# The up product of a two-layer feed-forward by Strassen's scheme: seven half-size products per strip in place of eight

## The reference, cut to what matters

```
h   = modulate(rms_norm(x), shift, scale)          # tokens x 1024
u   = h @ w_up                                      # 1024 x 5632: 2816 values, 2816 gates
u   = conv3(u)                                      # 3 taps along the tokens, per channel, zero at the ends
hid = value * silu(gate)                            # tokens x 2816
x   = x + gate_mod * (hid @ w_down)                 # 2816 x 1024
```

## Time and profile before

| | |
|---|---|
| median of 3 runs | 2685.11 us (2683.37 to 2685.4) |
| profiled execution | 2683.82 us, its span 2682.0 us |
| mean granted TensorE clock | 0.993 of full |
| TensorE busy | 2615.8 us, 98% |
| VectorE, ScalarE, GpSimd busy | 904.6, 613.0, 53.0 us |
| share of the chain that ended last | PE 95%, of the up loop (L1235) 15% |

### The profile page before, as it was taken

How to read it: one execution, slowest core, us unless ns; L and a number is a source line. 1 busy time by engine, 2 the same in 40 slices (tenths; PEclk the granted TensorE clock), 3 DMA queues, 4 the chain that set the end, 5 groups by cost and what they waited for, 6 DMA issues and landing times.

```text
span 2682.0 us, 29803 instructions
## 1 busy us (share of the span) xinstructions
PE 2615.8 (98%) x11774; PEld 1764.1 (66%) x11774; DVE 904.6 (34%) x1530; ACT 613.0 (23%) x1103; POOL 53.0 (2%) x42
## 2 busy tenths in 40 slices
PE   7999999999999899899999999999999999999999
PEld 3556656656656587666886444864444587889888
DVE  2236365365365512354125111232222014113321
ACT  3122212222121112243214000122221013113321
POOL 0000000000000100000000000000000000000000
PEclk9999999999999999999999999999999999999999
DMA  8443343333333223112520223222225232353572
GB/s 312 161 166 126 110 156 121 129 141 109 126 125 79 76 73 111 54 30 73 141 63 1 63 63 94 63 63 78 76 70 133 65 79 64 94 180 87 154 201 68
DMA packets 319714, 280.26 MB, mean 104 GB/s; under 512 B 27617, under 2 KB 298601, under 8 KB 319513
## 3 DMA queue, kind: packets, MB, share of 16 engines
q1 hardware_dynamic: 317882, 274.89, 33.4%
q0 software_dynamic: 1280, 4.20, 0.4%
q10 hardware_dynamic: 479, 0.13, 0.0%
HBM read 278.15 MB, written 1.05 MB: 104 GB/s over the span
## 4 chain that ended last, share of the span: by engine, by line
PE 95%; DVE 2%; DMA 1%; ACT 1%; SPq 0%; issue 0%; ACTq 0%; DVEq 0%
PE ps L660 17%; PE ps L1235 15%; PE ps L1158 9%; PE ps L1261 4%; PE ps L1251 4%; PE ps L669 4%; PE ps L707 4%; PE ps L1194 3%; PE ps L1170 3%; PE ps L427 2%; PE ps L853 2%; PE ps L807 2%; PE ps L789 2%; PE ps L374 2%; PE ps L1008 2%; PE ps L1221 1%
## 5 line engine op out<-in xcount | busy, mean ns | idle before, releaser
L660 PE MATMUL ps<-hT,ring_mem 128*128 128x512 f32 x1024 | 455.1, 598 | 1.7 <-ACT hT L440 1.7
L1235 PE MATMUL ps<-hT,ring_mem 128*128 128x512 f32 (+1 forms) x1280 | 413.2, 486 | 2.5 <-DMA ring_mem<-in_w_up_dram 2.5
L1235 PEld LDWEIGHTS ps<-hT,ring_mem 128*128 128x128 f32 x1280 | 243.1, 190 | 171.8 <-issue 155.3
L660 PEld LDWEIGHTS ps<-hT,ring_mem 128*128 128x128 f32 x1024 | 190.9, 191 | 234.8 <-issue 232.5
L1158 PE MATMUL ps<-hT,ring_mem 128*128 128x512 f32 (+1 forms) x768 | 250.3, 486 | 0.0
L1158 PEld LDWEIGHTS ps<-hT,ring_mem 128*128 128x128 f32 x768 | 145.9, 190 | 101.3 <-issue 91.4
L1986 DVE SCALAR_TENSOR_TENSOR arena<-ps,vecs,arena 128x510 f32<-128x510 f32 (+1 forms) x176 | 100.2, 611 | 304.6 <-ACT arena L1602 298.2
L707 PEld LDWEIGHTS ps<-arena,K_c 128*128 128x128 f32 x896 | 116.2, 194 | 34.3 <-issue 20.1
L707 PE MATMUL ps<-arena,K_c 128*128 128x128 f32 x896 | 120.1, 289 | 9.1 <-ACT K_c L1405 9.0
L1949 DVE TENSOR_TENSOR arena<-ps,arena 128x512 f32<-128x512 f32 (+1 forms) x48 | 26.8, 558 | 291.2 <-PE ps L1170 291.2
L1261 PE MATMUL ps<-arena,ring_mem 128*128 128x256 f32 (+1 forms) x704 | 116.1, 327 | 0.0
(11 more groups left out here) (246 smaller groups left out, 3090.5 us busy)
## 6 DMA issues: line engine op xcount, KB each, us to landing
ring_mem<-in_w_mod_dram SPq DMA_DIRECT2D x24, 2048.0 KB, 7.7
ring_mem<-in_w_up_dram SPq DMA_DIRECT2D x88, 512.0 KB, 4.9
ring_mem<-in_hg_w_in_dram SPq DMA_DIRECT2D x40, 1024.0 KB, 5.0
ring_mem<-in_w_in_dram SPq DMA_DIRECT2D x30, 1024.0 KB, 5.4
ring_mem<-in_w_down_dram SPq DMA_DIRECT2D x16, 1408.0 KB, 7.4
ring_mem<-in_ada_w_dram SPq DMA_DIRECT2D x8, 2048.0 KB, 7.8
ring_mem<-in_mla_w_in_dram SPq DMA_DIRECT2D x9, 1024.0 KB, 5.4
ring_mem<-in_hg_w_out_dram SPq DMA_DIRECT2D x8, 1024.0 KB, 12.0
```

Source lines behind the costliest of these rows:

```text
L660: mm = PE.matmul(bank, wj[:, k, m * 128:m * 128 + 128], hT[:, k, :], start=k == 0, stop=k == 7)
L1235: mm = PE.matmul(ps[:, 2 * j + m, 0:n], wj[:, k, m * 128:m * 128 + 128], hT[:, k, c0:T], start=k == 0, stop=k == 7)
```

## The change

For each strip the 1024 x 256 weights are cut into four blocks: a11 (input tiles k 0 to 3, values), a12 (k 4 to 7, values), a21 (k 0 to 3, gates), a22 (k 4 to 7, gates). The activations are cut in the same way: channels k 0 to 3 or 4 to 7, token half a or b. Seven products of half the depth and half the columns (P1 to P7, 4 matmuls each) replace the 16 matmuls over all tokens. Four of them take sums of weight blocks (S_up, two buffers), three differences of activations (T_up); hT's own tiles 0 to 3 of half b are overwritten by a difference.

- Activations: VectorE makes the four differences once per layer, when half b is ready (up_turned_vector).
- Weights: the sums 0 and 2 of strip f come from VectorE (first_sums, 4 x 128 columns each), for strips 0 and 1 from GpSimd; sums 1 and 3 always from GpSimd.
- Results: ScalarE copies P1 out of PSUM (into root), VectorE gathers the seven into the strip's values and gates, C_up (in SBUF, two buffers) by six additions. The middle and the outer taps then read C_up.
- Order: TensorE does P1 and P2 of strip f (plain), P4, P7, P5, P6, P3 (summed), and may be two strips ahead of the gathering (c_ready). VectorE's turn f is: first sums of f+2, gathering of f, taps of f-1, hidden of f-2. ScalarE's: copy P1 of f, taps of f, sigmoid of f-1; its taps of f wait for hidden f-2.
- Loops of up are written out for all engines. up has 4 slots at words 4096 to 12287 (loads on semaphores 2 to 5) in place of 2, so its slots 0 and 1 lie where out's slots 2 and 3 do.
- The banks of down's first pass are 0 to 3 (before 4 to 7), those of the halves are swapped, and the norms' sums of half b move to bank 7, so their squares wait for all of out's additions. The next layer's first keys wait for an addition of down more.

```
+        if s["total"] < s["slots"] * s["turns"]:
+            for n in range(s["total"]):
+                t, j = divmod(n, s["slots"])
+                if t or s["need"][j]:
+                    sp.wait_ge(self.used, s["first"] + n - s["slots"] + 1 if t else s["need"][j])
+                for dst, src in copies(j, t):
+                    sp.dma_start(dst, src).then_inc(self.loaded[s["first_slot"] + j], 16)
+            return
...
+        S_up = at(2 * 4 * 512).rearrange("p (b s k n) -> p b s k n", b=2, s=4, k=4)
+        T_up = at(3 * 4 * 256).rearrange("p (s k t) -> p s k t", s=3, k=4)
+        U_up = at(3 * 256).rearrange("p (s t) -> p s t", s=3)
+        P1_up = root
...
-            ring.stage(f"up{l}", 2, 2048, FT // 2, [2] * 2, first_slot=4, at=8192)
+            ring.stage(f"up{l}", 4, 2048, 6, [2] * 4, first_slot=2, at=4096, total=FT)
...
-            pe.wait_ge(x_added, x_part(l, "out", part, 1))
+            pe.wait_ge(x_added, x_part(l, "out", part, 1 if part == "_a" else 7))
...
+        def up_region(f, name, hw):
+            bank, part = {"P1": (0, 0), "P6": (0, 1), "P2": (1, 0), "P7": (1, 1), "P4": (2, 0), "P5": (2, 1), "P3": (3, 0)}[name]
+            return ps[:, f % 2 * 4 + bank, part * hw:part * hw + hw]
...
+            a, b, hw = up_halves(l)
+            def product(f, which, left, right, ready=None):
+                for k in range(4):
+                    if ready:
+                        ready(k)
+                    mm = PE.matmul(up_region(f, which, hw), left[:, k, :], right[:, k, 0:hw], start=k == 0, stop=k == 3)
+                return mm
+            def plain(f):
+                t, j = divmod(f, 4)
+                ring.wait_loaded(pe, name, j, t)
+                if f >= 2:
+                    pe.wait_ge(c_ready, FT * l + f - 1)
+                wj = strip(name, j, 8)
+                product(f, "P1", wj[:, 0:4, 0:128], hT[:, 0:4, a], (lambda k: wait_h(pe, f"ffn{l}_a", k)) if f == 0 else None)
+                product(f, "P2", wj[:, 4:8, 0:128], hT[:, 4:8, a], (lambda k: wait_h(pe, f"ffn{l}_a", 4 + k)) if f == 0 else None)
+            def summed(f):
+                wj = strip(name, f % 4, 8)
+                sums = S_up[:, f % 2]
+                p4 = lambda: product(f, "P4", wj[:, 4:8, 128:256], T_up[:, 2])
+                if f >= 1:
+                    p4()
+                if f >= 2:
+                    pe.wait_ge(first_sums_ready, (FT - 2) * l + f - 1)
+                else:
+                    pe.wait_ge(sums_ready, FT * l + f + 1)
+                if f == 0:
+                    pe.wait_ge(turned_ready, 4 * l + 1)
+                product(f, "P7", sums[:, 2], T_up[:, 0])
+                if f == 0:
+                    pe.wait_ge(turned_ready, 4 * l + 2)
+                product(f, "P5", sums[:, 0], hT[:, 0:4, b])
+                pe.wait_ge(sums_ready, FT * l + f + 1)
+                if f == 0:
+                    pe.wait_ge(turned_ready, 4 * l + 3)
+                product(f, "P6", sums[:, 1], T_up[:, 1])
+                mm = product(f, "P3", sums[:, 3], hT[:, 4:8, b])
+                if f == 0:
+                    pe.wait_ge(turned_ready, 4 * l + 4)
+                    mm = p4()
+                strip_used(mm)
+            plain(0)
+            ffn_norm_tensor(pe, l, "_b")
+            for f in range(FT):
+                if f == 0:
+                    plain(1)
+                    pe.wait_ge(root_ready, norm_no[f"ffn{l}_b"] + 1)
+                if f >= 2:
+                    plain(f)
+                summed(f)
...
+                    if j == 0 and k == 0:
+                        pe.wait_ge(c_ready, FT * l + FT - 1)
+                    mm = PE.matmul(ps[:, j, 0:n], wj[:, k, :], hid[:, k, 0:n], start=k == 0, stop=k == FT - 1)
                 strip_used(mm)
...
+            def gate(f):
+                act.wait_ge(conv_ready, FT * l + f + 1)
+                S.activation(sgf[:, f % 2, 0:n], acc[:, f % 2 * 2 + 1, 0:n], ACT.Sigmoid).then_inc(sf_ready, 1)
+            for f in range(FT):
+                act.wait_ge(strips_used, ring.stages[f"up{l}"]["first"] + f + 1)
+                S.activation(P1_up[:, 0:n // 2], up_region(f, "P1", n // 2), ACT.Copy).then_inc(p1_kept, 1)
+                act.wait_ge(c_ready, FT * l + f + 1)
+                if f >= 2:
+                    act.wait_ge(hid_ready, raised(FT * l + f - 1))
+                for part in range(2):
+                    S.activation(acc[:, f % 2 * 2 + part, 0:n], C_up[f % 2][:, part, 0:n], ACT.Identity,
+                                 scale=tap(l, 1, f, part)).then_inc(tap_ready, 1)
+                if f:
+                    gate(f - 1)
+            gate(FT - 1)
...
+        def up_turned_vector(dve, st, l):
+            a, b, hw = up_halves(l)
+            dve.wait_ge(h_ready, h_end[f"ffn{l}_b"])
+            V.tensor_tensor(T_up[:, 0, :, 0:hw], hT[:, 4:8, b], hT[:, 0:4, b], ALU.subtract).then_inc(turned_ready, 1)
+            V.tensor_tensor(hT[:, 0:4, b], hT[:, 0:4, b], hT[:, 0:4, a], ALU.subtract).then_inc(turned_ready, 1)
+            dve.wait_ge(turned_ready, 4 * l + 2)
+            V.tensor_tensor(T_up[:, 1, :, 0:hw], hT[:, 4:8, b], hT[:, 0:4, b], ALU.subtract).then_inc(turned_ready, 1)
+            dve.wait_ge(turned_ready, 4 * l + 3)
+            V.tensor_tensor(T_up[:, 2, :, 0:hw], hT[:, 4:8, a], T_up[:, 1, :, 0:hw], ALU.subtract).then_inc(turned_ready, 1)
...
+            def gather(f):
+                P = lambda which: up_region(f, which, hw)
+                U = lambda i: U_up[:, i, 0:hw]
+                C = C_up[f % 2]
+                dve.wait_ge(strips_used, ring.stages[f"up{l}"]["first"] + f + 1)
+                dve.wait_ge(p1_kept, FT * l + f + 1)
+                if f >= 2:
+                    dve.wait_ge(tap_ready, 2 * (FT * l + f - 1))
+                st.mark(V.tensor_tensor(U(0), P1_up[:, 0:hw], P("P6"), ALU.add))
+                V.tensor_tensor(C[:, 0, 0:hw], P1_up[:, 0:hw], P("P2"), ALU.add)
+                st.settle()
+                st.mark(V.tensor_tensor(U(1), U(0), P("P7"), ALU.add))
+                st.mark(V.tensor_tensor(U(2), U(0), P("P5"), ALU.add))
+                st.settle()
+                V.tensor_tensor(C[:, 1, 0:n].rearrange("p (s t) -> p s t", s=2), view(U(1), (0, 2), (1, hw)),
+                                ps[:, f % 2 * 4 + 2, 0:n].rearrange("p (s t) -> p s t", s=2), ALU.add)
+                V.tensor_tensor(C[:, 0, hw:n], U(2), P("P3"), ALU.add).then_inc(c_ready, 1)
+            def conv(f):
+                dve.wait_ge(tap_ready, 2 * (FT * l + f + 1))
+                dve.wait_ge(c_ready, FT * l + f + 1)
+                for k, (d0, s0) in ((0, (1, 0)), (2, (0, 1))):
+                    for part in range(2):
+                        dst = view(acc, (256, ns), (1, 255), at=(f % 2 * 2 + part) * T + d0)
+                        src = C_up[f % 2][:, part, 0:n].rearrange("p (s t) -> p s t", s=ns)[:, :, s0:s0 + 255]
+                        ins = V.scalar_tensor_tensor(dst, src, tap(l, k, f, part), dst, ALU.mult, ALU.add)
+                    if k == 0:
+                        st.link(ins)
+                    else:
+                        ins.then_inc(conv_ready, 1)
+            def hidden(f):
+                j = f % 2
+                dve.wait_ge(sf_ready, FT * l + f + 1)
+                st.link(V.tensor_tensor(acc[:, 2 * j, 0:n], acc[:, 2 * j, 0:n], acc[:, 2 * j + 1, 0:n], ALU.mult))
+                V.tensor_tensor(hid[:, f, 0:n], acc[:, 2 * j, 0:n], sgf[:, j, 0:n], ALU.mult).then_inc(hid_ready, 1)
+            def first_sums(f):
+                a11, _, a21, a22 = up_parts(l, f)
+                sums = S_up[:, f % 2]
+                wait_strip_f(dve, l, f - 2)
+                ring.wait_loaded(dve, f"up{l}", f % 4, f // 4)
+                V.tensor_tensor(sums[:, 0], a21, a22, ALU.add)
+                V.tensor_tensor(sums[:, 2], a11, a21, ALU.subtract).then_inc(first_sums_ready, 1)
+            for f in range(FT + 2):
+                if f + 2 < FT:
+                    first_sums(f + 2)
+                if f < FT:
+                    gather(f)
+                if 1 <= f <= FT:
+                    conv(f - 1)
+                if f >= 2:
+                    hidden(f - 2)
...
+                pool.wait_ge(y_ready, raised(8 * l + 8))
+                for f in range(FT):
+                    t, j = divmod(f, 4)
+                    ring.wait_loaded(pool, f"up{l}", j, t)
+                    sums = S_up[:, f % 2]
+                    a11, a12, a21, a22 = up_parts(l, f)
+                    if f >= 2:
+                        pool.wait_ge(first_sums_ready, (FT - 2) * l + f - 1)
+                    else:
+                        steps.mark(G.tensor_tensor(sums[:, 0], a21, a22, ALU.add))
+                        G.tensor_tensor(sums[:, 2], a11, a21, ALU.subtract)
+                        steps.settle()
+                    steps.link(G.tensor_tensor(sums[:, 1], sums[:, 0], a11, ALU.subtract))
```

(20 more changed lines are left out.)

114 lines of the change are left out of this document (44 added, 70 removed).

## The result

The changed kernel takes **2657.4 us** (median of 4, 2654.2 to 2658.6) against 2684.2 before (4 runs), a ratio of 0.990 [0.989, 0.991]. Forecast were 2656.0, range 2642 to 2680. The profiled execution took 2656.84 with a span of 2655.0, 27.0 under the span before. The total came out as forecast; several of its terms did not, so I go through the trace by the prediction's steps.

A forecast was written before the change was run, and what follows sets the result against it. TensorE's matmuls were taken to bound the up product. Gains of 52.6 us less 14.5 (starts), 7.5 (VectorE in layer 1) and 1.5 (end) gave 29.1 off the profiled 2683.8, so 2656 us, range 2642 to 2680.

The forecast's parts named there:

- TensorE's part: Up product's matmuls: 1232 smaller instructions per layer save 36.4 us in layer 0 and 13.7 in layer 1, together 50.1.
- The start: Start of each layer's up product: TensorE idles for differences, a transfer and GpSimd's hold on VectorE; 14.5 us lost, bounds 10 to 20.
- VectorE in layer 1: Layer 1's up loop: VectorE sets the pace, so the stage lasts 146.8 against 139.3 us, a loss of 7.5 us.
- the turn: VectorE's work per strip in layer 1's up loop: 5.56 + 0.2 + 0.5 + 0.6 = 6.9 us against TensorE's 6.33.
- My formula for the stage: Layer 1's up stage: 15.7 + 19 VectorE turns against TensorE's 139.3 us; VectorE bounds from a turn of 6.5.
- rival (a): Layer 1's up loop: VectorE stays hidden, its turn under 6.5 us; 2648 us, at the lower starts 2643; chance 0.22.
- GpSimd's operations: GpSimd's weight sums in the up loop: 1.1 us each, between bounds of 0.5 and 1.9; VectorE's taps lose 0.6.
- The end: Behind layer 1's up product: the down product waits 1.5 us for the last hidden strip; layer 0 loses nothing.
- The tables, the banks and the down strips: ScalarE's table loads, swapped banks and the down strips' loads behind up's: costed at nothing, at most 1 us for the banks.
- (b): Layer 1's up loop: VectorE's turn is about 8.0 us, from GpSimd operations of 1.6; 2677 us; chance 0.17.
- (c): Layer 1's up loop: VectorE's turn passes 8.4 us through GpSimd sums of about 2.1 or more; slower, 2705 at 2.6; chance 0.09.
- (d): Half-size products run slower, 0.118 for 0.113 us in layer 1, 1% in layer 0; 2660 us; counted within the forecast's 0.52.

The follow-up runs named there:

- experiment 2: The changed kernel with unused matmuls in TensorE's gaps (24 behind P1 and P2 of strip 1, 11 ahead of strip 0 in layer 1): 2651.4 us.
- experiment 4: The changed kernel with VectorE multiplying hidden f-2 at the head of its turn instead of the end: 2657.6 us.
- experiment 6: The changed kernel with all four weight sums of strips 2 to 21 on VectorE, none on GpSimd, in both layers: 2657.5 us.
- experiment 7: The changed kernel with sum 1 of strips 2 to 21 moved to VectorE, leaving GpSimd only sum 3: 2652.9 us.
- experiment 5: The changed kernel with GpSimd's two sums made twice per strip in layer 1 from strip 2 on: 2694.6 us, ratio 1.004 to the kernel before.

## Why the prediction was right, and where it was not

The total was right in part by luck: the mechanism that the forecast gave to layer 1's loop did not occur, and a cost that it did not have came in its place.

**TensorE's part: right.** A strip takes 12.08 us in layer 0 (forecast 12.11) and 6.25 in layer 1 (6.33); 22 of each are 265.8 and 137.6, a gain of 37.0 and 15.4 against 36.4 and 13.7. Per instruction layer 1 has 0.1117 us for the 0.113 that I took from the down product of before. The transfer's wait of 2.5 is gone as forecast.

**The start: the mechanism right, the sum too small.** Layer 0 idles 6.1 where 5.0 + 1 stood. Layer 1 waits 2.75 and 6.3 where 2.4, 4.1 and 2 stood: 15.2 in all, by the forecast's 14.5. What failed is that I let TensorE go on at full pace behind each gap. The lower clock cost 2.8 in layer 0 and 1.7 + 2.2 in layer 1, **6.7 us that no term held**; the unused matmuls of experiment 2 show the cause. The trace of before had a sign that I didn't look up, TensorE's own stretch behind its wait of 2.2 us near the end:

```profile
2675.60:2680.00 4.40, 2.52 (x8) 1.19 (x8) 1.67 (x6) 2.65 (x9) 0.00 (x0) 0.69 0.07 27
```

**VectorE in layer 1: wrong.** The step that failed is the turn, 6.9 forecast and 6.36 to 6.37 measured. The terms add up to 6.86 before rounding, 0.50 too much: 0.2 were waits that don't exist, 0.18 the gathering, 0.10 the hidden operations, 0.08 the first sums and their gap; against these the taps with GpSimd's hold were 0.06 longer than forecast (the hold is 0.76 for 0.6, the taps without it are shorter). My formula for the stage (15.7 + 19 turns, against TensorE's 139.3) came near where it could be tried: a turn of 6.76 (experiment 4) gives 4.8 us of loss, and 5.9 were measured; 8.30 gives 34, and 37 were measured; 6.48 (experiment 6) gives none, and 2.1 were measured, so the point from which VectorE bounds lies a little below my 6.5; 6.37 gives none, as the trace shows. I gave this case, rival (a), 0.22; its price of 2648 supposed that all else held. So **7.5 us that were to be lost were not**, and they stand against the 6.7 of the clock. Of the smaller errors, TensorE's part gave 2.3 more than forecast, the waits at the start took 0.7 more, the end 2.7 and all else 0.6. With about 1 us that is left between these terms and the account, this makes the 2.1 by which 27.0 falls short of 29.1.

**GpSimd's operations: nearly right.** 1.26 to 1.30 us for 1.1 where VectorE does not stand in their way, up to 1.50 where it does. My estimate of 1.12 from the Trainium skill ("GPSIMD Engine Reference", "Elementwise — side-by-side cycle accounting") is short by about as much; it scales the page's duration for 2048 elements down in proportion, and the measurement decides.

**The end: the wait right, its cause and size not.** 1.5 forecast, 2.1 of waiting measured, and again the clock behind it (0.59 for 3.8 us): 4.2 in all. Experiments 4 and 7 take 3.4 and 4.3 of it away. I had put the wait down to the time that the last strip needs; experiment 7 shows that a VectorE that does not lag leaves none.

**The tables, the banks and the down strips: right at nothing.** There is one table load per layer in up_scalar (L1662); everything else than the up product and its ends comes to 0.6 us.

**The rivals.** (b) and (c) need longer GpSimd sums than were measured; experiment 5 makes each sum twice and so gets (c)'s outcome, slower than before the change. (d), a worse pace of the half-size products, didn't occur outside the stretches of low clock.

## What to carry to other kernels

Price a gap in TensorE's work by its length and by the matmuls behind it: here 1.7 to 2.8 us more behind each gap of 2.75 to 6.3 us. When a product is recombined, look at what its first strip now waits for (the memory of its weights, a last normalisation): that was worth 9.5 us on top of the 27, by where four buffers lie. And before an engine's work is shared with GpSimd, see which of VectorE's operations it will lie beside: one sum beside operations that read PSUM was a gain of 4.5 us, two, of which one met the taps, were worth 2 us at most.
